# Moving one Ln and Exp of the first half's input norm behind the second half's high parts on ScalarE

## The chip, the cores and the metric

The kernel runs on one core of a Trainium2 chip. The metric is the time of one execution on the device in microseconds (us), as the median of several executions. The engines are TensorE (PE, matrix products), VectorE (DVE), ScalarE (ACT), GpSimd (POOL) and SyncE (SP, which starts transfers). Each works through its own list of instructions in order; between engines there are semaphores.

## The reference

Two transformer blocks run over 512 tokens of width 1024, in float32. At three places the output of a stage is normalised and added to the residual stream, and the new stream is normalised again as the input of the next dense stage. Cut to that:

```python
def rms_norm(x, g):
    xf = x.astype(jnp.float32)
    y = xf * lax.rsqrt(jnp.mean(xf * xf, axis=-1, keepdims=True) + EPS)
    return (y * g.astype(jnp.float32)).astype(x.dtype)

x = x + gate * rmsnorm(mixed @ w_out, g_post)                 # end of the first block
f = swiglu(rms_norm(h, g_ffn1_pre), w_gate, w_up, w_down)     # place A: its input norm
h = h + 0.5 * rms_norm(f, g_ffn1_post)
qkv = rms_norm(h, g_mix_pre) @ w_in                           # place B: its input norm
h = h + rms_norm(mixed @ w_out, g_mix_post)
f = swiglu(rms_norm(h, g_ffn2_pre), w_gate, w_up, w_down)     # place C: its input norm
```

The rest (retention, two attentions of the first block, stick-breaking and banded attention of the second, a gated projection at the end) is not touched.

## The kernel before

**Layout.** Activations lie feature by token: X is 8 tiles of 128 features by 512 tokens. A product in float32 is made of three products of high and low parts (`mm3`, lines 285 to 287): high by high, low by high, high by low. The high part is a rounded copy by ScalarE, the low part the difference by VectorE. Weights come as a stream of 512 KB chunks, four slots deep.

**Halves.** At a join of two stages the tokens are worked in two halves of 256, numbered on through the kernel: t = 0 and 1 at place A (before the first feed-forward), 2 and 3 at place B (before the projection of queries, keys and values of the second block), 4 and 5 at place C (before the second feed-forward). For each half t and each feature tile k:

- VectorE (`next_u`, lines 1106 to 1122), in rounds n: T of tile n = output times root (L1111), X of tile n-1 = new residual (L1115), UL of tile n-2 = low part (L1122). UL of tile k waits for ScalarE's UH of tile k.
- ScalarE (`next_hi`): UH of tile k = X times the gain (the high part), which waits for X of tile k, and then the square of X, into T2 or T3 in turn.
- GpSimd (`sum_n`, L519) adds the squares up, six additions for the half.
- TensorE takes UH and UL of tile k as soon as UL is there (`u_ready`: the wait on `nu_lo`).

**The root of the input norm** is not applied to the input. The products are made of the unnormalised X, and their result is multiplied by the root afterwards (DVE, T6). So the root may come late: `n_stats(t)` on TensorE (L1640 and L1642) sums the squares over the 128 partitions with two products into the half of bank B5 that belongs to t, and `n_rms(t)` on ScalarE makes Ln and then Exp of it into T6.

**TensorE's order** at A and C (`mlp_up`): four weight chunks on the first half (j = 0 to 3, each 24 products of 256 columns), `n_stats(t)`, then the same chunks on the second half, where j = 0 waits tile by tile for UL, with `n_stats(t + 1)` behind j = 1. Then the loop over the remaining chunks with 512 columns. Place B has the same pattern with the first four chunks of the projection.

**ScalarE's order** is written out by hand. `n_rms(t - 1)`, the root of the first half, stands in the middle of the second half's `next_hi`: behind tile 3 at A and C, behind tile 4 at B. It waits for `n_stats` of the first half. The root of the second half follows all eight tiles; at A and C a load of another function table and the first Silu come behind it.

Of the kernel before, what the change touches and what calls it, by code (L numbers as in the profile page):

```python
# [68 lines left out]
def build(nc, a):  # L69
    with ExitStack() as ctx:  # L70
# [77 lines left out]

        TAIL_AT = ((0, 44), (3, 47), (6, 50), (9, 53), (12, 56), (16, 19), (22, 25), (28, 60))
        TAIL_H = [hb(f"TAIL_H{m}", kb, [P, TAIL], F32R) for m, (kb, _) in enumerate(TAIL_AT)]  # L150
        TAIL_L = [hb(f"TAIL_L{m}", kb, [P, TAIL], F32R) for m, (_, kb) in enumerate(TAIL_AT)]

        EP = hb("EP", 0, [P, KT, SEQ])
# [88 lines left out]
        def wait(eng, s, value):  # L242

            if value > 0:
                eng.wait_ge(*((s.sem, s.base + value) if isinstance(s, Event) else (s, value)))
# [37 lines left out]
        def mm3(out, lh, ll, rh, rl, start, stop, **kw):  # L283
# [6 lines left out]
        E = {n: Event(n) for n in (  # L290
            "silu_c converted ada_dot gain_cols x_sq angle sines x_stats u_t u_hi u_lo "
            "y_copy y_sq y_sum y_st y_ln y_rstd y_t x_new nu_hi nu_lo n_sq n_sum n_st n_ln n_rstd half "
            "q_mul q_swap q_rot q_hi q_lo v_hi v_lo k_flat gates "
            "ret_s ret_p ret_hi ret_lo ret_pv gn_x gn_c gn_sq gn_g gn_v gn_ln gn_std gn_m gn_hi gn_lo "
            "cmp_h cmp_silu cmp_dup cmp_kv cmp_kh cmp_kl cmp_bd cmp_st cmp_sc cmp_s cmp_sub cmp_exp cmp_p cmp_t cmp_tc "
            "gate_cols "
            "sb_z sb_m sb_l sb_sp sb_spm sb_sph sb_spl sb_zz sb_p sb_pm sb_hi sb_lo sb_pv "
            "p5_q p5_hi p5_lo p5_vhi p5_vlo rt_tr rt "
# [32 lines left out]
        def cols_of(t):  # L331

            return slice(HALF * (t % 2), HALF * (t % 2) + HALF)
# [278 lines left out]
        def _(act):  # L612
            chain = Chain(act, "act_chain")

            def f(out, in_, func, **kw):
                return nc.scalar.activation(out, in_, func, **kw)  # L616

            def table_set(which):

                nc.scalar.add_instruction(mybir.InstLoadActFuncSet(  # L620
                    name=nc.get_next_instruction_name(), engine=mybir.EngineType.Activation, ins=[], outs=[],
                    act_func_set_id=which))

            def hi_of_weights(d):

                act.wait_ge(raw_here[d % SLOTS], 16 * (d // SLOTS + 1))
                if d in PHASE_OF:
                    phase, m = PHASE_OF[d]
                    hi = kept_weights(phase, m)[0]
                    if phase in ("d1", "d2"):  # L630
                        act.wait_ge(mm, d - m - (8 if m < 5 else 0))
                    f(hi[:, :], RAW[:, d % SLOTS, 0:hi.shape[1]], ACT.Copy).then_inc(w_hi, 1)
                else:
                    f(WH[:, d % SLOTS, :], RAW[:, d % SLOTS, :], ACT.Copy).then_inc(w_hi, 1)
# [20 lines left out]
            def n_rms(t):  # L655

                wait(act, E["n_st"], 2 * t + 2)
                E["n_ln"].mark(f(T[6][:, cols_of(t)], B[5][:, cols_of(t)], ACT.Ln, scale=1.0 / DM, bias=EPS))
                wait(act, E["n_ln"], t + 1)
                E["n_rstd"].mark(f(T[6][:, cols_of(t)], T[6][:, cols_of(t)], ACT.Exp, scale=-0.5))  # L660

            def next_hi(t, k, scale):

                h = cols_of(t)
                wait(act, E["x_new"], 8 * t + k + 1)
                if scale is None:
                    E["nu_hi"].mark(f(UH[:, k, h], X[:, k, h], ACT.Copy))
                    return
                E["nu_hi"].mark(f(UH[:, k, h], X[:, k, h], ACT.Copy, scale=scale[:, k:k + 1]))
                c = t  # L670
                if k >= 2:
                    wait(act, E["n_sum"], 6 * c + max(1, k - 2))
                E["n_sq"].mark(f(T[2 + k % 2][:, h], X[:, k, h], ACT.Square))
# [212 lines left out]
            def mlp_up(d0, n0, t, scale):  # L886

                for k in range(KT):
                    next_hi(t, k, scale)
                    if k == 3:  # L890
                        n_rms(t - 1)
                n_rms(t)
                table_set(SILU_SET)
                for j in range(4):
                    if j >= 2:
                        hi_of_weights(d0 + j + 2)
                    if j % 2 == 0:
                        act.wait_ge(f_g, n0 + j // 2 + 1)
                        f(T[2 + j // 2][:, :], T[j // 2][:, :], ACT.Silu).then_inc(f_s, 1)
                    else:  # L900
                        act.wait_ge(f_h, n0 + j // 2 + 1)
                        f(HH[:, j // 2, :], T[5][:, :], ACT.Copy).then_inc(f_hh, 1)
                c4 = d0 // 4
                with act.Fori(1, 11) as i:
                    for j in range(4):
                        nxt = (j + 2) % 4
                        act.wait_ge(raw_here[nxt], i * 16 + 16 * (c4 + 1 + (j >= 2)))
                        f(WH[:, nxt, :], RAW[:, nxt, :], ACT.Copy).then_inc(w_hi, 1)
                        if j % 2 == 0:
                            act.wait_ge(f_g, i * 2 + (n0 + j // 2 + 1))  # L910
                            f(T[2 + j // 2][:, :], T[j // 2][:, :], ACT.Silu).then_inc(f_s, 1)
                        else:
                            act.wait_ge(f_h, i * 2 + (n0 + j // 2 + 1))
                            f(HH[:, i * 2 + j // 2, :], T[5][:, :], ACT.Copy).then_inc(f_hh, 1)
# [26 lines left out]

            project_out("p2", D_P2, 0, VECS[:, V_F1PRE:V_F1PRE + 8], D_F1)
            mlp_up(D_F1, 0, 1, VECS[:, V_F1PRE:V_F1PRE + 8])
            mlp_down(D_D1, 2, VECS[:, V_MPRE:V_MPRE + 8])
            y_rms(3)
            for k in range(KT):
                next_hi(3, k, VECS[:, V_MPRE:V_MPRE + 8])
                if k == 4:
                    n_rms(2)
            n_rms(3)  # L950


# [97 lines left out]
            for p in range(4):  # L1050
                heads_hi(BDN, p, T[4:6], MBH)
            project_out("p6", D_P6, 4, VEC2[:, V2_F2PRE:V2_F2PRE + 8], D_F2)
            mlp_up(D_F2, 22, 5, VEC2[:, V2_F2PRE:V2_F2PRE + 8])
            mlp_down(D_D2, 6, None)

# [13 lines left out]
            for n in range(17):  # L1069
# [4 lines left out]
                if n < 16:  # L1074
                    m, t = n % 8, 8 + n // 8
# [542 lines left out]
        def _(pe):  # L1618
# [17 lines left out]
            def n_stats(t):  # L1636

                h, c = cols_of(t), t
                wait(pe, E["n_sum"], 6 * c + 6)
                E["n_st"].mark(mat(B[5][:, h], ONES, T[4][:, h], start=True, stop=False))  # L1640
                wait(pe, E["n_sq"], 8 * c + KT)
                E["n_st"].mark(mat(B[5][:, h], ONES, T[3][:, h], start=False, stop=True))  # L1642
# [280 lines left out]
            def mlp_up(phase, d0, n0, t):  # L1923
                for j in range(4):
                    between = None
                    if j == 0:
                        between = lambda: y_stats(t + 1)
                    half_chunk(d0 + j, bank_of(phase, j), *u_in, t, None, between=between,
                               ready=u_ready(t) if j == 0 else None)
                n_stats(t)  # L1930
                for j in range(4):
                    half_chunk(d0 + j, B[j], *u_in, t + 1, mm, ready=u_ready(t + 1) if j == 0 else None)
                    if j == 1:
                        n_stats(t + 1)
                with pe.Fori(1, 11) as i:
                    for j in range(4):
                        pe.wait_ge(w_lo, i * 4 + (d0 + j + 1))
                        pe.wait_ge((f_g, f_u)[j % 2], i * 2 + (n0 + j // 2 - 1))
                        for k in range(KT):
                            ins = mm3(B[j][:, :], wtile(WH, j, k), wtile(WL, j, k), UH[:, k, :], UL[:, k, :], k == 0, k == KT - 1)  # L1940
                        ins.then_inc(mm, 1)
# [41 lines left out]
            for j in range(4):  # L1983
                half_chunk(D_P5 + j, bank_of("p5", j), *u_in, 2, None, ready=u_ready(2) if j == 0 else None,
                           between=(lambda: y_stats(3)) if j == 0 else None)
            n_stats(2)
            for j in range(4):
                half_chunk(D_P5 + j, B[j], *u_in, 3, mm, ready=u_ready(3) if j == 0 else None)
# [252 lines left out]
```

## Time and profile before

| | us |
|---|---|
| median of 3 runs | 1522.67 (1521.61 to 1522.95) |
| the profiled execution's own time | 1521.06 |
| its span in the trace | 1519.3 |
| TensorE busy | 1462.5 (96%) |
| VectorE busy | 838.9 (55%) |
| ScalarE busy | 683.7 (45%) |
| GpSimd busy | 203.6 (13%) |

The span runs from the first to the last instruction; the execution's time is 1.8 us longer. The chain of work that ended last is 82% TensorE, so time is won where TensorE waits or runs at half of its clock. The three places lie at about 420 us (A), 794 us (B) and 1089 us (C) of the span.

### The profile page before, as it was taken

What the parts mean: (1) busy time and instruction counts of PE and PEld (TensorE: products, weight loads), DVE (VectorE), ACT (ScalarE), POOL (GpSimd) and SP (SyncE); (2) the same over time, 40 slices, a digit from 0 to 9 for tenths busy, and PEclk for the clock granted to TensorE, in tenths of its full rate; (3) what the DMA queues carried; (4) which work ended last, traced back from release to release, by engine and by line L of the source; (5) the groups of instructions that cost most, each with busy time, mean ns of one, the idle gap of its engine ahead of it and who ended that gap; (6) DMA issues with size and microseconds to landing.
All of it is one profiled execution on the core that took longest, in us unless ns stands there. A gap on an engine that the chain in (4) does not pass through costs nothing.

```text
span 1519.3 us, 22041 instructions
## 1 busy us (share of the span) xinstructions
PE 1462.5 (96%) x8524; PEld 1234.3 (81%) x8524; DVE 838.9 (55%) x1455; ACT 683.7 (45%) x1302; POOL 203.6 (13%) x319
## 2 busy tenths in 40 slices
PE   7999998999999999999999999989999999999997
PEld 5887875778988888888898777769888888888996
DVE  6688646776654444432285566574754444422374
ACT  4556436676532222221363566676432222322463
POOL 0000000443400000000140223451300000000121
PEclk9999999899999999999999999999999999999998
DMA  9542440004023333333404211503033333332321
GB/s 367 202 152 85 124 153 10 1 2 167 2 84 97 97 97 97 97 97 97 144 10 167 70 56 42 167 16 97 19 107 97 97 97 97 97 111 90 119 84 56
DMA packets 42148, 146.71 MB, mean 97 GB/s; under 512 B 4673, under 2 KB 7121, under 8 KB 41682
## 3 DMA queue, kind: packets, MB, share of 16 engines
q1 hardware_dynamic: 37986, 128.99, 26.5%
q0 software_dynamic: 3072, 15.71, 2.8%
q8 instruction: 54, 0.88, 0.2%
q10 hardware_dynamic: 1008, 0.89, 0.2%
q14 instruction: 28, 0.23, 0.0%
HBM read 141.39 MB, written 4.19 MB: 96 GB/s over the span
## 4 chain that ended last, share of the span: by engine, by line
PE 82%; DVE 10%; ACT 4%; issue 2%; DMA 1%; POOL 0%; DVEq 0%; SPq 0%; ACTq 0%; POOLq 0%
PE B L285 22%; PE B L287 21%; PE B L286 21%; PE CROW_P L285 3%; PE CROW_P L287 3%; PE CROW_P L286 3%; PE B L1772 2%; ACT T L616 1%; PE B L2008 1%; PE CROW_P L1851 1%; DVE WADA L1137 1%; DVE WL L1104 1%; DVE AL L1370 1%; DVE X L1115 1%; PE CROW_P L1751 1%
## 5 line engine op out<-in xcount | busy, mean ns | idle before, releaser
L285 PE MATMUL B<-UH,WH 128*128 128x512 f32 (+1 forms) x1008 | 378.0, 375 | 12.0 <-DVE UL L1122 6.3
L287 PE MATMUL B<-UH,WL 128*128 128x512 f32 (+1 forms) x1008 | 373.9, 371 | 0.0
L286 PE MATMUL B<-UL,WH 128*128 128x512 f32 (+1 forms) x1008 | 373.9, 371 | 0.0
L616 ACT ACTIVATE WH<-RAW 128x1024 fp32r<-128x1024 f32 x174 | 182.6, 1052 | 118.7 <-DMA RAW<-in_stream 110.3
L285 PEld LDWEIGHTS B<-UH,WH 128*128 128x128 f32 x1008 | 191.6, 190 | 47.9 <-DVE UL L1122 8.7
L286 PEld LDWEIGHTS B<-UL,WH 128*128 128x128 f32 x1008 | 191.7, 190 | 31.9
L287 PEld LDWEIGHTS B<-UH,WL 128*128 128x128 f32 x1008 | 191.5, 190 | 32.0
L1104 DVE TENSOR_TENSOR WL<-RAW,WH 128x1024 fp32r<-128x1024 f32 x94 | 116.1, 1240 | 143.8 <-ACT WH L616 143.7
L1447 DVE TENSOR_TENSOR WL<-RAW,WH 128x1024 fp32r<-128x1024 f32 x80 | 98.1, 1226 | 76.7 <-ACT WH L616 73.9
L616 ACT ACTIVATE T<-B 128x256 f32<-128x256 f32 (+5 forms) x186 | 86.3, 464 | 118.0 <-PE B L287 64.3
L510 POOL TENSOR_TENSOR T<-T,T 128x256 f32<-128x256 f32 x60 | 54.7, 912 | 548.8 <-ACT T L616 547.9
L616 ACT ACTIVATE T<-T 128x512 f32<-128x512 f32 (+3 forms) x131 | 68.7, 526 | 131.8 <-DVE T L1451 119.2
L616 ACT ACTIVATE HH<-T 128x512 f32 (+1 forms) x44 | 27.8, 632 | 190.7 <-DVE T L1456 183.8
L286 PE MATMUL B<-HL,WH 128*128 128x512 f32 x192 | 74.8, 390 | 0.0
L285 PE MATMUL B<-HH,WH 128*128 128x512 f32 x192 | 74.8, 390 | 0.0
L287 PE MATMUL B<-HH,WL 128*128 128x512 f32 x192 | 74.8, 389 | 0.0
L285 PE MATMUL B<-UH,KEPT_H 128*128 128x256 f32 (+1 forms) x220 | 66.5, 302 | 1.6 <-DVE KEPT_L L1102 1.6
L1453 DVE TENSOR_TENSOR T<-B,T 128x512 f32<-128x512 f32 x40 | 27.7, 692 | 71.7 <-PE B L287 71.7
L286 PE MATMUL B<-UL,KEPT_H 128*128 128x256 f32 (+1 forms) x220 | 66.0, 300 | 0.0
L287 PE MATMUL B<-UH,KEPT_L 128*128 128x256 f32 (+1 forms) x220 | 65.8, 299 | 0.0
L1370 DVE TENSOR_TENSOR AL<-CROW_P,AH 128x128 fp32r<-128x128 f32 (+3 forms) x96 | 42.7, 484 | 18.1 <-ACT AH L616 17.7
L616 ACT ACTIVATE AH<-CROW_P 128x128 fp32r<-128x128 f32 (+3 forms) x96 | 38.2, 436 | 23.3 <-PE CROW_P L1851 22.6
(419 smaller groups left out, 3161.2 us busy)
## 6 DMA issues: line engine op xcount, KB each, us to landing
RAW<-in_stream SPq DMA_DIRECT2D x202, 512.0 KB, 3.6
WADA<-in_w_ada SPq DMA_DIRECT2D x8, 1024.0 KB, 16.6
RAW<-in_stream SPq DMA_DIRECT2D x16, 384.0 KB, 3.3
WADA<-in_w_ada SPq DMA_DIRECT2D x2, 2048.0 KB, 11.1
W<-in_w POOLq DMA_DIRECT2D x2, 2048.0 KB, 11.7
X<-in_x SPq DMA_DIRECT2D x2, 1024.0 KB, 11.0
DECAY<-in_decay POOLq DMA_DIRECT2D x1, 2048.0 KB, 9.3
X<-in_x POOLq DMA_DIRECT2D x2, 1024.0 KB, 8.2
```

Source lines behind the costliest of these rows:

```text
L285: nc.tensor.matmul(out, lh, rh, start=start, stop=False, **kw)
L286: nc.tensor.matmul(out, lh, rl, start=False, stop=False, **kw)
L287: return nc.tensor.matmul(out, ll, rh, start=False, stop=stop, **kw)
L510: E["y_sum"].mark(nc.gpsimd.tensor_tensor(T[7][:, h], T[8][:, h] if k == 1 else T[7][:, h], T[8 + k % 2][:, h], ALU.add))
L616: return nc.scalar.activation(out, in_, func, **kw)
L1104: tt(WL[:, d % SLOTS, :], RAW[:, d % SLOTS, :], WH[:, d % SLOTS, :], ALU.subtract).then_inc(w_lo, 1)
L1115: E["x_new"].mark(stt(X[:, k, h], T_RING[k % 4][:, h], gain[:, k:k + 1], X[:, k, h], ALU.mult, ALU.add))
L1137: E["ada_dot"].mark(stt(WADA[:, m, :], WADA[:, m, :], 1.0, (CROW_P if m < 2 * KT else CROW)[:, :], ALU.mult, ALU.mult, accum_out=DOTS[:, m ...
L1370: tag["lo"].mark(tt(AL2[:, u % 4, 0:(i + 1) * P], PT_BANK[s][:, 0:(i + 1) * P], AH2[:, u % 4, 0:(i + 1) * P], ALU.subtract))
L1447: tt(WL[:, nxt, :], RAW[:, nxt, :], WH[:, nxt, :], ALU.subtract).then_inc(w_lo, 1)
L1453: tt(T[4][:, :], B[j][:, :], T[6][:, :], ALU.mult).then_inc(f_u, 1)
L1772: ins = [mat(outs[s], fixed[s][x], moving[s][y], start=start and x + y == 0, stop=stop and x == 1) for s in range(2)]
```

## The change

At A and C (`mlp_up` of ScalarE) and at B, `n_rms` of the first half moves from the middle of the second half's tiles to behind the eighth, directly ahead of `n_rms` of the second half. On TensorE `n_stats` of an odd t, which writes the other half of the same bank B5, gets a wait for the Ln of the first half. No instruction is added or removed besides that wait.

```diff
@@ ScalarE, mlp_up (places A and C)
                 for k in range(KT):
                     next_hi(t, k, scale)
-                    if k == 3:
-                        n_rms(t - 1)
+                n_rms(t - 1)
                 n_rms(t)
@@ ScalarE, place B
             for k in range(KT):
                 next_hi(3, k, VECS[:, V_MPRE:V_MPRE + 8])
-                if k == 4:
-                    n_rms(2)
+            n_rms(2)
             n_rms(3)
@@ TensorE, n_stats
                 wait(pe, E["n_sum"], 6 * c + 6)
+                if t % 2 == 1:
+                    wait(pe, E["n_ln"], t)
                 E["n_st"].mark(mat(B[5][:, h], ONES, T[4][:, h], start=True, stop=False))
```

**ScalarE at place A.** UH_51<-X_49 is a high part, T2_177 or T3_178<-X_49 its square, T6_181<-B5 the Ln and T6_181<-T6_181 the Exp of a root. Before, from the square of tile 3 on:

```order
L616 ACTIVATE T3_178<-X_49 128x256 [waits n_sum]
L616 ACTIVATE T6_181<-B5 128x256 [waits n_st]
L616 ACTIVATE T6_181<-T6_181 128x256 [waits n_ln]
L616 ACTIVATE UH_51<-X_49,VECS_205 128x256 [waits x_new]
L616 ACTIVATE T2_177<-X_49 128x256 [waits n_sum]
L616 ACTIVATE UH_51<-X_49,VECS_205 128x256 [waits x_new]
L616 ACTIVATE T3_178<-X_49 128x256 [waits n_sum]
L616 ACTIVATE UH_51<-X_49,VECS_205 128x256 [waits x_new]
L616 ACTIVATE T2_177<-X_49 128x256 [waits n_sum]
```

and now, from the same square to the Exp of the second half's root:

```order
L616 ACTIVATE T3_178<-X_49 128x256 [waits n_sum]
L616 ACTIVATE UH_51<-X_49,VECS_205 128x256 [waits x_new]
L616 ACTIVATE T2_177<-X_49 128x256 [waits n_sum]
L616 ACTIVATE UH_51<-X_49,VECS_205 128x256 [waits x_new]
L616 ACTIVATE T3_178<-X_49 128x256 [waits n_sum]
L616 ACTIVATE UH_51<-X_49,VECS_205 128x256 [waits x_new]
L616 ACTIVATE T2_177<-X_49 128x256 [waits n_sum]
L616 ACTIVATE UH_51<-X_49,VECS_205 128x256 [waits x_new]
L616 ACTIVATE T3_178<-X_49 128x256 [waits n_sum]
L616 ACTIVATE T6_181<-B5 128x256 [waits n_st]
L616 ACTIVATE T6_181<-T6_181 128x256 [waits n_ln]
L616 ACTIVATE T6_181<-B5 128x256 [waits n_st]
```

The Ln, with its wait for `n_st`, stood between the square of tile 3 and the high part of tile 4; now four pairs of high part and square stand there, and both roots follow them. Place C reads the same, and at place B three pairs move ahead in place of four.

**TensorE at place A, the last products of j = 1 and `n_stats(1)`.** Before:

```order
L285 MATMUL B1<-UH_51,WH_56 128x256
L286 MATMUL B1<-UL_52,WH_56 128x256
L287 MATMUL B1<-UH_51,WL_57 128x256
L1640 MATMUL B5<-T4_179,CONST_199 128x256 [waits n_sum]
L1642 MATMUL B5<-T3_178,CONST_199 128x256 [waits n_sq]
L285 MATMUL B2<-UH_51,WH_56 128x256 [waits w_lo]
```

and now:

```order
L285 MATMUL B1<-UH_51,WH_56 128x256
L286 MATMUL B1<-UL_52,WH_56 128x256
L287 MATMUL B1<-UH_51,WL_57 128x256
L1640 MATMUL B5<-T4_179,CONST_199 128x256 [waits n_ln,n_sum]
L1642 MATMUL B5<-T3_178,CONST_199 128x256 [waits n_sq]
L285 MATMUL B2<-UH_51,WH_56 128x256 [waits w_lo]
```

Nothing moves; the first product of the sum waits for `n_ln` too.

## Rows read from the trace of the kernel before

**Rows 1.** The page: busy time of the engines, and the chain that ended last by engine.

```profile
PE 1462.5 (96%) x8524; PEld 1234.3 (81%) x8524; DVE 838.9 (55%) x1455; ACT 683.7 (45%) x1302; POOL 203.6 (13%) x319
...
PE 82%; DVE 10%; ACT 4%; issue 2%; DMA 1%; POOL 0%; DVEq 0%; SPq 0%; ACTq 0%; POOLq 0%
```

**Rows 2.** All waits of PE: operand and line, releaser, us in total, times, longest.

```profile
PE B L285 <- DVE UL L1122: 6.3, 8, 1.5
```

**Rows 3.** Timeline of ScalarE at place A: start, us, engine, line, operation, [idle <- releaser].

```profile
417.33 0.40 ACT L616 ACTIVATE T<-X 128x256 f32<-128x256 f32 x1
421.44 0.38 ACT L616 ACTIVATE T<-B 128x256 f32<-128x256 f32 x1 [3.70 <-PE B L1642]
...
422.17 0.50 ACT L616 ACTIVATE UH<-X,VECS 128x256 fp32r<-128x256 f32 x1
...
432.39 0.38 ACT L616 ACTIVATE T<-B 128x256 f32<-128x256 f32 x1 [5.82 <-PE B L1642]
```

**Rows 4.** Timeline of VectorE at place A.

```profile
417.54 0.47 DVE L1115 SCALAR_TENSOR_TENSOR X<-T,GC,X 128x256 f32<-128x256 f32 x1
417.93 0.96 DVE L1122 SCALAR_TENSOR_TENSOR UL<-X,VECS,UH 128x256 fp32r<-128x256 f32 x1
...
419.15 0.47 DVE L1115 SCALAR_TENSOR_TENSOR X<-T,GC,X 128x256 f32<-128x256 f32 x1
422.70 0.48 DVE L1122 SCALAR_TENSOR_TENSOR UL<-X,VECS,UH 128x256 fp32r<-128x256 f32 x1 [3.08 <-ACT UH L616]
...
426.29 0.69 DVE L1122 SCALAR_TENSOR_TENSOR UL<-X,VECS,UH 128x256 fp32r<-128x256 f32 x1 [0.18 <-ACT UH L616]
```

**Rows 5.** Timeline of GpSimd at place A.

```profile
417.81 0.79 POOL L519 TENSOR_TENSOR T<-T,T 128x256 f32<-128x256 f32 x1 [1.21 <-ACT T L616]
```

**Rows 6.** Timeline of TensorE at place A.

```profile
421.05 0.47 PE L285 MATMUL B<-UH,WH 128*128 128x256 f32 x1
...
425.38 0.39 PE L285 MATMUL B<-UH,WH 128*128 128x256 f32 x1 [1.52 <-DVE UL L1122]
...
431.32 0.60 PE L1640 MATMUL B<-T,CONST 128*128 128x256 f32 x2
...
432.00 0.47 PE L285 MATMUL B<-UH,WH 128*128 128x256 f32 x1
...
437.82 0.28 PE L287 MATMUL B<-UH,WL 128*128 128x256 f32 x1
439.04 0.49 PE L285 MATMUL B<-UH,WH 128*128 128x512 f32 x1 [0.94 <-DVE WL L1104]
```

**Rows 7.** Windows at place A: length, busy PE, PEld, DVE, ACT, POOL, granted clock, DMA share.

```profile
426.00:428.00 2.00, 1.92 (x8) 1.68 (x8) 0.81 (x2) 0.57 (x2) 0.70 (x1) 0.50 0.00 0
428.00:430.00 2.00, 2.00 (x14) 2.00 (x13) 0.00 (x0) 0.00 (x0) 0.00 (x0) 0.70 0.43 90
```

**Rows 8.** Timeline of ScalarE, VectorE and TensorE at place B.

```profile
794.36 0.38 ACT L616 ACTIVATE T<-B 128x256 f32<-128x256 f32 x1 [2.02 <-PE B L1642]
...
792.63 0.95 DVE L1115 SCALAR_TENSOR_TENSOR X<-T,SC,X 128x256 f32<-128x256 f32 x1
...
793.97 0.47 PE L285 MATMUL B<-UH,WH 128*128 128x256 f32 x1
...
801.66 0.60 PE L1640 MATMUL B<-T,CONST 128*128 128x256 f32 x2
```

**Rows 9.** Timeline of VectorE and TensorE at place C.

```profile
1087.72 0.47 DVE L1115 SCALAR_TENSOR_TENSOR X<-T,VECS,X 128x256 f32<-128x256 f32 x1
...
1089.07 0.47 PE L285 MATMUL B<-UH,WH 128*128 128x256 f32 x1
...
1099.77 0.60 PE L1640 MATMUL B<-T,CONST 128*128 128x256 f32 x2
```

**Rows 10.** Waits of PE from 440 us on.

```profile
PE CROW_P L1851 <- DVE AL L1370: 6.4, 10, 2.5
```

**Rows 11.** A window in the attention stage, between B and C.

```profile
1016.00:1024.00 8.00, 6.10 (x52) 5.82 (x53) 4.19 (x9) 3.72 (x8) 4.78 (x4) 0.57 0.23 68
```

## The prediction

> **What bounds the kernel now.** I read the page first. TensorE is busy for 96% of the span and makes up 82% of the chain that ended last [rows 1], so an edit on ScalarE is worth only what it takes from TensorE's waits, or from stretches at half clock. The list of TensorE's waits comes second. One entry is what this edit can touch: 6.3 us in 8 waits of a product for UL, the low part that VectorE makes of the next input [rows 2]. UL waits for the high part UH on ScalarE. So third, the timelines of the three places.
>
> At place A the second half begins on TensorE at 421.05 [rows 6]. ScalarE has squared tile 3 at 417.33 to 417.73 and then stands for 3.70 us, until `n_stats(0)` has let the Ln go at 421.44 [rows 3]. It stands behind TensorE's whole first half, though X of tile 4 was ready at 417.54 + 0.47 = 418.01 [rows 4]. Ln and Exp pass, UH of tile 4 starts at 422.17 [rows 3], UL of tile 4 at 422.70 after 3.08 us of idle time, UL of tile 7 ends at 426.29 + 0.69 = 426.98 [rows 4]. TensorE waits for these tiles (1.52 us for tile 5) [rows 6], and behind these waits its granted clock goes to 0.50, the lower level of 1.2 GHz, in the window from 426, and has a mean of 0.70 in the one from 428 [rows 7]; 2 x 0.50 + 2 x 0.30 = 1.6 us are lost by it.
>
> What that costs is read off one pair of stretches. From the start of the second half to `n_stats(1)` there are 48 products of 256 columns: 431.32 - 421.05 = 10.27 us. The next 48 of the same shape, from 432.00 to the last one, which starts at 437.82 and takes 0.12 until the next could start, need 5.94 us without a wait and at full clock [rows 6]. So **4.33 us** at A are waits and half clock. The same difference is 801.66 - 793.97 - 5.94 = **1.75 us** at B [rows 8] and 1099.77 - 1089.07 - 5.94 = **4.76 us** at C [rows 9]. The most that the edit can win there is 10.84 us.
>
> **The moved root.** Four pairs of UH and square are freed from the wait at A and C, three at B. ScalarE needs 0.50 + 0.40 us for a pair at most [rows 3], under the beat of VectorE, so VectorE sets the pace. Its beat is a round of T, X and UL, from X to X: 419.15 - 417.54 = 1.61 us, with one of the three instructions slowed to 0.96 us [rows 4]. With UH in time, UL of tile 4 comes one beat after that of tile 3: 417.93 + 1.61 = 419.54; tile 5 at 421.15. The last rounds lack T, then X too: between UL of tile 5 and UL of tile 6 lies X alone, between 6 and 7 nothing. At 0.39 us for an instruction (417.93 - 417.54) or 0.88 for a slowed one (0.96 less the overlap of 0.08), with two additions of GpSimd still falling on them, tile 6 starts near 422.3, tile 7 near 423.1 and ends near **423.6**. That is 4.45 us after the start of X of tile 5, at 419.15.
>
> TensorE wants tile 7 of its first chunk 2.7 us after its start: of the 48 products that take 5.94 us, 27 are still to come then, at (437.82 - 432.00) / 47 = 0.12 each. That is 421.05 + 2.70 = 423.75. It is there. Gain at A: 4.3 us, waits and clock together, because TensorE then runs without a pause from the first half on.
>
> At C the same X starts at 1087.72 against TensorE's 1089.07 [rows 9], 1.35 us ahead in place of 1.90. Tile 7 ends at 1087.72 + 4.45 = 1092.17, wanted at 1091.77: 0.4 us stay. Gain 4.76 - 0.4 = 4.4 us. At B, X of tile 5 starts at 792.63 and TensorE's half at 793.97 [rows 8]; only tiles 5 to 7 were held there, for 2.02 us. Tile 7 ends near 797.08, wanted at 796.67: again 0.4 us stay. Gain 1.75 - 0.4, about 1.3 us.
>
> **Why VectorE does not go faster still.** The instruction of 0.96 us at 417.93 lies beside GpSimd's addition of 417.81 to 418.60 [rows 4, 5] and ends 0.29 us behind it; others of the same kind take 0.47. By the Trainium skill, page Advanced Engine Details and Errata, section GPSIMD Details, GpSimd shares a read and a write interface with VectorE and conflicts with VectorE's instructions that have two inputs in SBUF. The trace agrees (0.47 against 0.96 us). This speaks against the change: squares that come earlier send GpSimd's additions into VectorE's rounds. By that rule applied to every instruction the gain is that of the first rival, by the beat of the trace it is the one above.
>
> **The root itself now comes later.** Ln and Exp of the first half come behind the square of tile 7: at A near 423.6, against 421.44 before. Nobody wants them there: VectorE multiplies by the root only after both halves, and it waits for the second half's Exp. Whoever is queued behind them on ScalarE is the second half's Ln, which starts at 432.39 after 5.82 us of idle time [rows 3]; the moved two take 422.17 - 421.44 = 0.73 us together [rows 3], inside that idle time. No transfer is issued among the moved steps and no queue of SP or GpSimd is passed.
>
> **The added wait.** `n_stats(1)` waits for the Ln of the first half, ended by about 424.1 at A. TensorE comes there at 421.05 + 5.94 = 427.0. Cost 0, with about 3 us in hand; behind it on TensorE stand j = 2 and 3 and the whole loop, so if that cover went, each us late would cost 1 us. Bounds: 0 here, and no gain either, since a wait cannot help.
>
> **What is late next.** After A, TensorE waits 0.94 us for the low part of the next weights at 439.04 [rows 6]. Their chain (Ln, Exp, table, Silu, high part, low part) starts with `n_stats(1)` [rows 3, 6], so it moves forward with it and stays 0.94 us. Weight transfers are issued at the end of TensorE's chunks and move too. The gain stays until the end, since behind each place the chain is TensorE's [rows 1].
>
> **Sum.** 4.3 + 1.3 + 4.4 = 10.0 us. The profiled execution took 1521.06; 1511.1 after. Its time is 1.6 below the median of the runs, 1522.67, against which I forecast: **1512.7 us**. Lower bound 10.84 less, 1511.8, and lower only by the clock elsewhere.
>
> **Rivals.**
>
> 1. VectorE is slowed throughout. If all seven instructions from UL of tile 4 on took 0.88, tile 7 would end at 419.54 + 7 x 0.88 = 425.7 at A: 1.95 us of waits remain, and the drop of the clock, 1.6 us [rows 7], may remain. Gain at A 4.33 - 1.95 - 1.6 = 0.8, at C 0.7, at B 0: 1521.2, within 0.2%. For it: [rows 4]. Against: GpSimd has only some 3 additions of 0.79 us left, for three slowed instructions, not seven. A middle form, where one of A and C keeps waits of 1 us and the drop of the clock, gives a gain of 5 to 8: 1514.7 to 1517.7.
> 2. The clock falls elsewhere. All that lies behind A moves by 4 to 10 us. Waits that passed at full clock could bring it down. A drop like that at A costs 1.6 us, and one that vanishes gives as much back. For it: behind A, TensorE has 10 waits of up to 2.5 us for the low parts of the attention weights, 6.4 us in all [rows 10]; one of them is followed by a drop already, a mean of 0.57 over 8 us [rows 11], so 3.4 us lost, which may come out 1.6 shorter or longer. Three more drops: 1517.5. The side where the kernel gets slower is this mechanism with 8 or more new drops, 8 x 1.6 = 12.8 against 10: 1525.5. It decides from 6 drops on, where the gain is gone. Against: the waits do not get longer by the change, and A's drop came behind a row of waits, not one. The Trainium skill says, on the page TensorE: Matmul & The Clock Gate, part 1, that the chip's watch over TensorE's activity runs free and doesn't start with the kernel, so that the same code meets it at another phase. By that, one drop more or less, 1511.1 or 1514.3, is ordinary; no row here shows it.
> 3. The added wait bites: if the squares or sums of the second half came 3 us later than I have them, TensorE would stand at `n_stats`. That would cost gain, not more: n_stats waits for the last squares in any case, 0.4 us before that Ln.
> 4. The edit does nothing, since UL was late for another reason (X itself late). Then tile 4's UL would not have followed 0.02 us behind UH [rows 3, 4]: 422.17 + 0.50 against 422.70. Nearly excluded.
>
> **How the numbers follow.** My forecast with its own range, 1510.5 to 1514.5: 0.74. Middle form of the first rival, 1514.5 to 1518: 0.12. Drops or gains of the clock elsewhere that leave the forecast but stay faster: 0.07. No measurable gain: 0.04. Slower: 0.03. The range from 1509.8 to 1517.0 leaves out about 0.15. A measurement of this kernel can tell about 0.2%, 3 us, from no change. Faster by more than that: 0.93, within it 0.04, slower 0.03.
>
> **What would show it.** In the profile after: no idle time of ScalarE ahead of UH of tile 4 but for X; UL of tile 7 ending about 2.5 us after the start of TensorE's second half at A and 3.1 at B and C (before: 5.9 at A); `n_stats(1)` near 5.95 us behind that start, near 6.35 at B and C; no window below full clock at A and C; the wait of 0.94 us unchanged. I would be wrong if the beat of VectorE from tile 4 on is 2 us or more, if the clock still drops at A or C, or if new drops stand behind them.

## The result

The changed kernel takes 1511.82 us (median of 4 runs, 1510.92 to 1512.90) against 1522.14 us of the kernel before in the same comparison. The ratio is 0.9937 with a 95% interval from 0.9924 to 0.9949: **0.63% faster**, 9.6 us by the ratio, while the medians lie 10.3 us apart. Forecast were 1512.7 us and 10.0 us. The profiled execution's span is 1509.6 us against 1519.3.

The page of the kernel after, in answer to [rows 1]:

```profile
PE 1456.9 (97%) x8524; PEld 1230.8 (82%) x8524; DVE 838.6 (56%) x1455; ACT 683.7 (45%) x1302; POOL 204.3 (14%) x319
...
PE 81%; DVE 12%; ACT 4%; issue 2%; POOL 0%; DVEq 0%; ACTq 0%; POOLq 0%
```

TensorE is busy 5.6 us less and its share of the chain is one point lower.

ScalarE at place A after the change, in answer to [rows 3] (timeline: start, us, engine, line, operation, idle time before it and what ended that):

```profile
417.27 0.40 ACT L616 ACTIVATE T<-X 128x256 f32<-128x256 f32 x1
417.98 0.51 ACT L616 ACTIVATE UH<-X,VECS 128x256 fp32r<-128x256 f32 x1 [0.31 <-DVE X L1113]
...
422.48 0.51 ACT L616 ACTIVATE UH<-X,VECS 128x256 fp32r<-128x256 f32 x1 [0.46 <-DVE X L1113]
422.90 0.40 ACT L616 ACTIVATE T<-X 128x256 f32<-128x256 f32 x1
423.20 0.36 ACT L616 ACTIVATE T<-B 128x256 f32<-128x256 f32 x1
...
428.17 0.38 ACT L616 ACTIVATE T<-B 128x256 f32<-128x256 f32 x1 [4.16 <-PE B L1642]
```

The square of tile 3 at 417.27 is followed by the high part of tile 4 at 417.98, as soon as X is there; it was 422.17 before. The first half's Ln stands at 423.20, behind all tiles, and the second half's at 428.17, after 4.16 us of idle time.

VectorE, in answer to [rows 4], and TensorE, in answer to [rows 6], both at A; then TensorE's first product of the loop behind it:

```profile
417.47 0.47 DVE L1113 SCALAR_TENSOR_TENSOR X<-T,GC,X 128x256 f32<-128x256 f32 x1
...
419.09 0.96 DVE L1113 SCALAR_TENSOR_TENSOR X<-T,GC,X 128x256 f32<-128x256 f32 x1
...
422.37 1.35 DVE L1120 SCALAR_TENSOR_TENSOR UL<-X,VECS,UH 128x256 fp32r<-128x256 f32 x2
```

```profile
420.99 0.47 PE L285 MATMUL B<-UH,WH 128*128 128x256 f32 x1
...
423.38 0.39 PE L285 MATMUL B<-UH,WH 128*128 128x256 f32 x1
...
427.11 0.60 PE L1640 MATMUL B<-T,CONST 128*128 128x256 f32 x2
...
434.82 0.49 PE L285 MATMUL B<-UH,WH 128*128 128x512 f32 x1 [0.94 <-DVE WL L1102]
```

The low parts of tiles 6 and 7 lie in one row that ends at 423.72; before, tile 7 ended at 426.98. TensorE's half starts at 420.99, its sum at 427.11: 6.12 us in place of 10.27. The product at 423.38 is the first of tile 6; it starts 0.17 us behind the one ahead of it, where 0.12 is the pace, so TensorE barely waits any more. The wait of 0.94 us for the next weights has not changed. The two windows behind, in answer to [rows 7], are at full clock (the last three columns are the granted clock, the share of the DMA engines and GB/s):

```profile
424.00:426.00 2.00, 2.00 (x19) 2.00 (x18) 0.00 (x0) 0.01 (x1) 0.00 (x0) 1.00 0.39 55
426.00:428.00 2.00, 2.00 (x16) 1.89 (x15) 0.00 (x0) 0.00 (x0) 0.00 (x0) 1.00 0.55 215
```

Places B and C, in answer to [rows 8, 9], TensorE at B, VectorE at B, TensorE at C:

```profile
789.74 0.47 PE L285 MATMUL B<-UH,WH 128*128 128x256 f32 x1
...
792.69 0.39 PE L285 MATMUL B<-UH,WH 128*128 128x256 f32 x1 [0.44 <-DVE UL L1120]
...
796.41 0.60 PE L1640 MATMUL B<-T,CONST 128*128 128x256 f32 x2
```

```profile
788.40 0.96 DVE L1113 SCALAR_TENSOR_TENSOR X<-T,SC,X 128x256 f32<-128x256 f32 x1
...
791.68 1.35 DVE L1120 SCALAR_TENSOR_TENSOR UL<-X,VECS,UH 128x256 fp32r<-128x256 f32 x2
```

```profile
1083.39 0.47 PE L285 MATMUL B<-UH,WH 128*128 128x256 f32 x1
...
1086.34 0.39 PE L285 MATMUL B<-UH,WH 128*128 128x256 f32 x1 [0.45 <-DVE UL L1120]
...
1090.07 0.60 PE L1640 MATMUL B<-T,CONST 128*128 128x256 f32 x2
```

B takes 6.67 us in place of 7.69, C 6.68 in place of 10.70. Each keeps one wait of 0.44 or 0.45 us.

The span falls apart into stretches that can be compared one by one. In this table, made from TensorE's rows of each trace, A, B and C are the 48 products from the start of a second half to its sum; "A to B" and "B to C" lie between, "to end" behind C.

| kernel | start of A | A | A to B | B | B to C | C | to end | start of A to end |
|---|---|---|---|---|---|---|---|---|
| before | 421.05 | 10.27 | 362.65 | 7.69 | 287.41 | 10.70 | 419.53 | 1098.25 |
| after | 420.99 | 6.12 | 362.63 | 6.67 | 286.98 | 6.68 | 419.53 | 1088.61 |
| e1_a_and_c | 420.89 | 6.14 | 362.64 | 7.68 | 286.58 | 6.67 | 419.50 | 1089.21 |
| e2_b_alone | 425.50 | 10.67 | 362.65 | 6.69 | 286.56 | 10.23 | 419.60 | 1096.40 |
| e4_filled_wait | 421.11 | 9.35 | 362.65 | 7.68 | 287.55 | 9.35 | 419.51 | 1096.09 |
| e3_short_sums | 420.18 | 5.94 | 362.66 | 5.94 | 286.82 | 5.94 | 419.52 | 1086.82 |
| e5_late | 421.13 | 6.12 | 362.66 | 6.65 | 286.96 | 6.66 | 419.52 | 1088.57 |
| e6_later | 421.39 | 9.49 | 362.71 | 10.04 | 287.10 | 10.04 | 419.93 | 1099.31 |
| e8_behind_5 | 420.31 | 6.42 | 362.63 | 6.69 | 287.31 | 6.67 | 419.57 | 1089.29 |
| e7_weights_first | 422.86 | 6.14 | 361.45 | 6.66 | 286.34 | 6.67 | 418.38 | 1085.64 |

From the start of A's second half to the end the change saves 9.64 us: 4.15 at A, 1.02 at B, 4.02 at C, 0.43 between B and C, 0.02 in the rest.

### The profile page after: what moved, and what is told of

Read it like the earlier page. It is cut to its first block, busy times and chain, and to the rows that moved or that the text cites. A ratio compares the mean times of both kernels' runs of the same rounds, so it can differ in the third digit from the quotient of the medians.

```text
span 1509.6 us, 22044 instructions
## 1 busy us (share of the span) xinstructions
PE 1456.9 (97%) x8524; PEld 1230.8 (82%) x8524; DVE 838.6 (56%) x1455; ACT 683.7 (45%) x1302; POOL 204.3 (14%) x319
## 4 chain that ended last, share of the span: by engine, by line
PE 81%; DVE 12%; ACT 4%; issue 2%; POOL 0%; DVEq 0%; ACTq 0%; POOLq 0%
PE B L285 21%; PE B L286 21%; PE B L287 21%; PE CROW_P L285 3%; PE CROW_P L286 3%; PE CROW_P L287 3%; PE B L1772 2%; PE B L2008 1%; DVE WADA L1135 1%; PE CROW_P L1851 1%; ACT T L616 1%; DVE X L1113 1%; DVE UL L1120 1%; DVE WL L1102 1%; DVE T L1109 1%
## 5 line engine op out<-in xcount | busy, mean ns | idle before, releaser
L1456 DVE TENSOR_TENSOR HL<-T,HH 128x512 f32 x40 | 27.7, 693 | 36.6 <-ACT HH L616 36.6
## 6 DMA issues: line engine op xcount, KB each, us to landing
X<-in_x SPq DMA_DIRECT2D x2, 1024.0 KB, 10.7
```

What stands on the lines that cost most here:

```text
L1456: tt(HL[:, i * 2 + j // 2, :], T[5][:, :], HH[:, i * 2 + j // 2, :], ALU.subtract).then_inc(f_hl, 1)
```

## The experiments

**Each place by itself.** Theory: every place gives back its own waits and its own drop of the clock. Rival: the gain is one place's, or the clock's elsewhere. First the change at A and C alone; the hunk of `mlp_up` and the wait on TensorE stay, and at B:

```diff
                 next_hi(3, k, VECS[:, V_MPRE:V_MPRE + 8])
-            n_rms(2)
+                if k == 4:
+                    n_rms(2)
             n_rms(3)
```

> The root is moved at places A and C only; place B is as before. Theory (each place gives back its own waits and clock drop): the profile after gives 4.15 us at A and 4.02 at C, read as the shorter way from the start of TensorE's second half to its sum, so 8.2 us less than before, a ratio near 0.9946. Rival (the gain is one place's, or the clock's elsewhere): clearly less than 7 or more than 9.5 us.

Measured: 1512.68 us, ratio 0.9933 (0.9915 to 0.9950). TensorE at B in that trace:

```profile
789.67 0.47 PE L285 MATMUL B<-UH,WH 128*128 128x256 f32 x1
...
793.62 0.38 PE L285 MATMUL B<-UH,WH 128*128 128x256 f32 x1 [1.13 <-DVE UL L1121]
...
797.35 0.60 PE L1641 MATMUL B<-T,CONST 128*128 128x256 f32 x2
```

B takes 7.68 us with its old wait, A and C take 6.14 and 6.67 as in the changed kernel. A and C give 4.13 + 4.03 = 8.16 us, as the theory says. From the start of A to the end it is 9.04 us less, since the stretch from B to C came out 0.83 us shorter. That goes with a shorter drop of the clock there, a mean of 0.79 over 8 us where [rows 11] have 0.57:

```profile
1010.00:1018.00 8.00, 5.26 (x45) 4.64 (x45) 3.21 (x7) 4.27 (x9) 3.98 (x5) 0.79 0.21 56
```

The times by themselves would not decide: by the ratio it is 10.2 us, with an interval from 7.6 to 12.9, which holds the theory's 8.2 as well as the rival's "more than 9.5". The stretches decide.

Then the change at B alone:

```diff
                     next_hi(t, k, scale)
-                n_rms(t - 1)
+                    if k == 3:
+                        n_rms(t - 1)
                 n_rms(t)
```

> The root is moved at place B only. Theory: 1.0 us less than before (7.69 against 6.67 us in the profile after), a ratio near 0.9993, too small to be told from no change in the time, but to be read in the trace as 6.7 us from the start of the second half to the sum; the drops of the clock behind A and C stay. Rival (the moved root at B costs, as it comes later): 7.7 us or more in that stretch.

Measured: B takes 6.69 us in the trace, 1.00 less, as expected, and A and C keep 10.67 and 10.23 us. The time was 1518.37 us, ratio 0.9973 (0.9958 to 0.9989). That is 4 us less than before where 1.0 was expected, and the trace doesn't show such a gain: in the profiled execution, which took 1523.62 us, the way from A to the end is only 1.85 us shorter, 0.85 of it between B and C. The mean granted clock of each run tells more. The two runs of e2_b_alone at 0.983 took 1523.62 and 1523.90 us, those of the kernel before at the same clock 1524.71 to 1525.37; at 0.988 and 0.989 it is 1517.18 to 1519.08 against 1519.97 to 1520.19. So at a like clock the change at B is worth some 1 to 2 us, and the rest of the 4 us is that seven of its nine runs had a clock of 0.987 or more, against five of the nineteen of the kernel before. Why it was so stays open; the last section shows where executions differ by that much.

**What the clock has to do with it.** The kernel before, but TensorE is kept busy inside its long wait:

```diff
+            def filled(t, d):
+                def ready(k):
+                    if k == 5:
+                        keep_clock(6, WH[:, d % SLOTS, 0:SEQ], B[6])
+                    wait(pe, E["nu_lo"], 8 * t + k + 1)
+                return ready
...
-                    half_chunk(d0 + j, B[j], *u_in, t + 1, mm, ready=u_ready(t + 1) if j == 0 else None)
+                    half_chunk(d0 + j, B[j], *u_in, t + 1, mm, ready=filled(t + 1, d0) if j == 0 else None)
```

> The kernel before, with the root where it was, but TensorE is given six products of 512 columns into an unused bank between tiles 4 and 5 of the second half's first chunk at A and C, about 6 x 0.23 = 1.4 us inside its wait of 1.52 us. Theory (the clock falls because TensorE waits there): no window under full clock behind A and C, the 48 products take about 8.7 us in place of 10.3 and 9.1 in place of 10.7, in all 3.2 us less than before, ratio 0.998. Rival (the clock would fall anyway, or for another reason): the drop stays and the time is the same or up to 0.5 us longer.

Measured: 1518.93 us, ratio 0.9970 (0.9960 to 0.9980). By the times that is 4 to 5 us, more than the 3.2 expected and than the 2.16 that the way from A to the end shows; the surplus is not explained, as at e2_b_alone. TensorE at A (the filling, tiles 5, 6 and 7, the sum) and two windows behind it:

```profile
423.76 1.53 PE L1648 MATMUL CROW_P<-WH 128*128 128x512 f32 x6
425.46 0.39 PE L285 MATMUL B<-UH,WH 128*128 128x256 f32 x1 [0.16 <-DVE UL L1122]
...
426.25 0.38 PE L285 MATMUL B<-UH,WH 128*128 128x256 f32 x1 [0.17 <-DVE UL L1122]
...
427.12 0.38 PE L285 MATMUL B<-UH,WH 128*128 128x256 f32 x1 [0.25 <-DVE UL L1122]
...
430.46 0.60 PE L1640 MATMUL B<-T,CONST 128*128 128x256 f32 x2
```

```profile
426.00:428.00 2.00, 1.57 (x11) 1.29 (x11) 0.89 (x2) 0.66 (x2) 0.79 (x1) 1.00 0.00 0
428.00:430.00 2.00, 2.00 (x19) 2.00 (x19) 0.00 (x0) 0.00 (x0) 0.00 (x0) 1.00 0.59 143
```

The six products fill the wait, 0.16 us of it is left ahead of tile 5, and both windows are at full clock where [rows 7] shows 0.50 and 0.70. So the drop comes from TensorE's waiting, as the theory says. But the stretch falls to 9.35 us, not to the expected 8.7: at A the drop cost 10.27 - 9.35 = 0.92 us, at C 10.70 - 9.35 = 1.35. The remaining 9.35 - 5.94 = 3.41 us are waits, the filled one among them. I had counted the granted clock's whole shortfall, 1.6 us, as lost; a part of it falls where TensorE waits for tiles 6 and 7 anyway. At full clock these waits are 0.17 and 0.25 us (the rows above). In the kernel before they stand at C, where the clock falls only by tile 7,

```profile
1094.19 0.39 PE L285 MATMUL B<-UH,WH 128*128 128x256 f32 x1 [0.17 <-DVE UL L1122]
...
1095.07 0.58 PE L285 MATMUL B<-UH,WH 128*128 128x256 f32 x1 [0.26 <-DVE UL L1122]
```

while at A, where it falls ahead of tile 6, the trace shows no wait at tiles 6 and 7: the slower products fill that time. 0.17 + 0.26 = 0.43 us is as much as the drop costs more at C than at A. So the price depends on the moment of the drop: in e2_b_alone the two figures stand the other way round, 10.67 us at A and 10.23 at C.

**What sets VectorE's beat.** The changed kernel, with GpSimd's additions of five of the second half's tiles cut to 16 columns; it leaves most of those sums out:

```diff
                 h, c = cols_of(t), t
                 wait(pool, E["n_sq"], 8 * c + k + 1)
...
+                if t % 2 == 1 and k > 1:
+                    h = slice(h.start, h.start + 16)
                 E["n_sum"].mark(nc.gpsimd.tensor_tensor(T[4][:, h], T[2][:, h] if k == 1 else T[4][:, h],
```

> The changed kernel; GpSimd's additions of the squares of tiles 2 to 6 of the second halves go over 16 of the 256 columns only, so most of those sums of squares are left out. They are no longer beside VectorE's instructions. Theory (VectorE's beat is set by GpSimd's additions, 0.96 in place of 0.47 us for one instruction each): the beat from X to X falls from 1.61 to about 1.15 us, tile 7 is ready in time at B and C too, the stretch takes 5.95 us at all three places, so 1.4 to 1.7 us less than the changed kernel. Rival (VectorE is slowed by ScalarE or by its own writes): the beat stays at 1.6 us and the time is that of the changed kernel.

Measured: 1511.22 us, ratio 0.9926 (0.9907 to 0.9946); its runs go from 1508.79 to 1514.76, too far apart to show 1.5 us, so the trace has to. An addition on GpSimd, and X of tiles 4 and 5 and the last low part on VectorE, at A, where TensorE's half starts at 420.18:

```profile
418.68 0.28 POOL L521 TENSOR_TENSOR T<-T,T 128x16 f32<-128x16 f32 x1 [0.85 <-ACT T L618]
```

```profile
417.27 0.47 DVE L1115 SCALAR_TENSOR_TENSOR X<-T,GC,X 128x256 f32<-128x256 f32 x1
...
418.40 0.47 DVE L1115 SCALAR_TENSOR_TENSOR X<-T,GC,X 128x256 f32<-128x256 f32 x1
...
420.24 0.49 DVE L1122 SCALAR_TENSOR_TENSOR UL<-X,VECS,UH 128x256 fp32r<-128x256 f32 x1 [0.18 <-ACT UH L618]
```

The addition takes 0.28 us in place of 0.79 [rows 5], no instruction of VectorE takes 0.96 any more, the beat is 418.40 - 417.27 = 1.13 us in place of 1.61, and tile 7 is ready 0.55 us after TensorE's start. All three stretches take 5.94 us, exactly the figure without a wait. So what the change leaves at B and C, 0.73 and 0.74 us, and the 0.18 at A, goes back to GpSimd's additions, beside which VectorE's instructions are slowed. The three places give 1.65 us together, as expected, and from A to the end it is 1.79.

**How late the root may be.** The changed kernel with copies on ScalarE ahead of the moved root, at all three places, 5 and then 15 of them:

```diff
+            def idle(n):
+                for _ in range(n):
+                    chain.done(f(T[5][:, 0:HALF], X[:, 0, 0:HALF], ACT.Copy))
...
+                idle(5)
                 n_rms(t - 1)
                 n_rms(t)
...
+            idle(5)
             n_rms(2)
             n_rms(3)
```

> The changed kernel, with 5 copies of 256 columns on ScalarE, each waited for, ahead of the moved root at all three places: about 2 to 2.5 us. Theory (TensorE comes to the sum of the second half 3.5 us after the Ln of the first half at A, 3.5 at B and C): the delay is hidden, the time is that of the changed kernel within 0.3 us. Rival (the late root costs at once): 2 us more at each place, 6 in all.

> The same with 15 copies, about 6.5 to 7 us. Theory: the Ln comes some 3 to 3.5 us after TensorE reaches the sum, which waits for it by the added wait, so about 3 us more at each place, 9 to 10 in all, plus up to 1.6 us a place if the clock falls: as slow as the kernel before, or slower by up to 5 us. Rival (nobody waits for that Ln): the time of the changed kernel.

Measured with 5: 1511.35 us, ratio 0.9937 (0.9922 to 0.9953), and stretches of 6.12, 6.65 and 6.66 us. With 15: 1524.20 us, ratio 1.0016 (1.0002 to 1.0030). ScalarE at A with 5 copies (they share a row with the last square), then ScalarE and TensorE at A with 15:

```profile
423.04 2.52 ACT L616 ACTIVATE T<-X 128x256 f32<-128x256 f32 x6
425.59 0.39 ACT L616 ACTIVATE T<-B 128x256 f32<-128x256 f32 x1
...
428.31 0.39 ACT L616 ACTIVATE T<-B 128x256 f32<-128x256 f32 x1 [1.89 <-PE B L1648]
```

```profile
423.30 7.02 ACT L616 ACTIVATE T<-X 128x256 f32<-128x256 f32 x16
430.35 0.39 ACT L616 ACTIVATE T<-B 128x256 f32<-128x256 f32 x1
...
430.88 0.67 PE L1646 MATMUL B<-T,CONST 128*128 128x256 f32 x2 [3.21 <-ACT T L616]
```

With 5 copies the Ln comes at 425.59 and costs nothing. With 15 it comes at 430.35, and TensorE's sum of the second half waits for it 3.21 us, 3.20 at B and 3.21 at C. The stretches are 3.37 us longer than in the changed kernel at each place, 10.1 in all, of 10.7 in the whole. The granted clock stays at 1.00 in every window behind A, but falls behind B and C, to a mean of 0.79 over the 8 us from 803.60 and from 1100.70: the same wait of 3.2 us brings a drop at two places and none at the third. The added wait is real, its cover ends where forecast, and behind it a us costs about one. The root's own lateness costs nothing by itself.

**Where behind the wait.** The root behind tile 5 at all three places:

```diff
                     next_hi(t, k, scale)
-                n_rms(t - 1)
+                    if k == 5:
+                        n_rms(t - 1)
                 n_rms(t)
```

> The root of the first half is put behind tile 5 at all three places, not behind tile 7. In the profile after, the square of tile 5 ends at 420.9 at A, and the first half's sum is there at 421.4. Theory (what costs is that ScalarE stands while X is ready): the Ln waits 0.5 us, Ln and Exp take 0.8, the high part of tile 6 comes 0.9 us later than in the changed kernel, TensorE waits 0.3 to 0.9 us more at each place: 1 to 2.5 us slower than the changed kernel, 7 to 8.5 faster than before. Rival (any place between tiles is as good once the wait is gone): the time of the changed kernel.

Measured: 1511.54 us, ratio 0.9939 (0.9924 to 0.9955). ScalarE and VectorE at A, where TensorE's half starts at 420.31:

```profile
420.70 0.38 ACT L616 ACTIVATE T<-B 128x256 f32<-128x256 f32 x1 [0.48 <-PE B L1644]
...
421.44 0.50 ACT L616 ACTIVATE UH<-X,VECS 128x256 fp32r<-128x256 f32 x1
```

```profile
421.97 0.48 DVE L1122 SCALAR_TENSOR_TENSOR UL<-X,VECS,UH 128x256 fp32r<-128x256 f32 x1 [0.19 <-ACT UH L616]
422.67 0.67 DVE L1122 SCALAR_TENSOR_TENSOR UL<-X,VECS,UH 128x256 fp32r<-128x256 f32 x1 [0.22 <-ACT UH L616]
```

The steps came as I had them: the Ln waits 0.48 us, the high part of tile 6 starts 1.13 us behind TensorE's start, against 421.20 - 420.99 = 0.21 in the changed kernel. The price did not: A takes 6.42 us, 0.30 more, B and C 6.69 and 6.67, nothing more. My estimate of 1 to 2.5 us was wrong, and the gain of 9.3 us by the ratio is more than the 7 to 8.5 I had. The late high parts also make their squares late, GpSimd's additions leave VectorE's rounds, and the low part of tile 6 takes 0.48 us, where in the changed kernel the low parts of tiles 6 and 7 took 1.35 us together. What VectorE waits for ScalarE it mostly gains on GpSimd. So the gain lies in leaving the long wait, not in the exact place behind it.

**A faster version.** The waits of 0.94, 0.85 and 0.93 us behind the three places are for the first weights of the next loop. ScalarE and VectorE stand idle ahead of the second half's root, so their part in these weights can go there:

```diff
@@ ScalarE, mlp_up
                 n_rms(t - 1)
+                hi_of_weights(d0 + 4)
                 n_rms(t)
...
-                    if j >= 2:
+                    if j == 3:
                         hi_of_weights(d0 + j + 2)
@@ VectorE, project_out
+                lo_of_weights(up + 4)
                 wait(dve, E["n_rstd"], t + 2)
@@ VectorE, mlp_up
-                    if j >= 2:
+                    if j == 3:
                         lo_of_weights(d0 + j + 2)
@@ place B, ScalarE (and the same with lo_of_weights on VectorE)
-                if c >= 2:
+                if c == 1:
+                    hi_of_weights(D_P5 + 4)
+                if c >= 3:
                     hi_of_weights(D_P5 + c + 2)
```

> The changed kernel, with the high and low part of the first weights of the next loop made while ScalarE and VectorE stand idle ahead of the second half's root (A and C), or one step earlier (B). Theory (the waits of 0.94, 0.93 and 0.85 us for these weights are only an order on ScalarE and VectorE): they vanish, 2.0 to 2.7 us less than the changed kernel; the root comes 0.5 us later at A and C, and its chain has that much room behind it. Rival (the chain through Silu is what the loop waits for next): the waits turn into others for the second chunk and the time stays.

Measured: 1509.44 us, ratio 0.9921 (0.9907 to 0.9935), the fastest of all kernels here that compute everything. In the same comparison e5_late and e8_behind_5 took 1511.35 and 1511.54, 1.9 and 2.1 us more; the intervals of the ratios overlap, so here too the stretches are the firmer evidence. ScalarE and VectorE at A:

```profile
429.90 1.06 ACT L616 ACTIVATE WH<-RAW 128x1024 fp32r<-128x1024 f32 x1 [4.00 <-DMA RAW<-in_stream]
430.87 0.37 ACT L616 ACTIVATE T<-B 128x256 f32<-128x256 f32 x1
...
430.99 1.23 DVE L1105 TENSOR_TENSOR WL<-RAW,WH 128x1024 fp32r<-128x1024 f32 x1 [5.39 <-ACT WH L616]
```

The high part waits for its transfer and delays the second half's Ln: it starts 430.87 - 429.00 = 1.87 us behind the start of TensorE's sum, where it was 428.17 - 427.11 = 1.06 in the changed kernel, so 0.8 us later and not 0.5. The low part is ready at 432.2, and TensorE takes it at 435.62 without a wait. The three waits are gone and no other takes their place: A to B 1.18 us shorter, to the end 1.15, B to C 0.64, and from the start of A to the end 2.97 us less than the changed kernel. The theory held; the rival (the chain through Silu) did not show.

## Why the prediction was right

**The bound and the most that could be won.** The 5.94 us without a wait were read right: three stretches of e3_short_sums took exactly that.

**The moved root.** Forecast 4.3 + 1.3 + 4.4 = 10.0 us; measured 4.15 + 1.02 + 4.02 = 9.19, and 0.43 by a shorter stretch between B and C. Each term was a little too large, for two reasons that lie in TensorE's side of the comparison. At A, tile 7 ended at 423.72 where 423.6 was forecast, so the walk along VectorE's beat was right in its end (the low part of tile 4 came 0.43 us later than in the walk, at 419.97, because X of tile 5 took 0.96 us). But I compared tile 7 alone with TensorE. At B it was tile 6 that came late: its low part, the first of the two in the row at 791.68, released the product at 792.69, which by TensorE's own pace was wanted 18 products behind 789.74, at 792.08. That is 0.61 us late; the row shows 0.44 because it counts from the end that the profile gives the product ahead, 0.28 us behind its start, while the next can start after 0.12. Besides, the first product behind a wait takes 0.22 us until the next starts and not 0.12, and so the stretches lost 0.73. So "0.4 us stay" should have been 0.73 at both places, and "it is there" at A 0.18.

**The time itself.** The forecast of 1512.7 us came within 0.9 us of the median. That is in part luck: the runs of one kernel differ by several us for a reason ahead of place A (last section), the stretches give 9.64 us and the medians 10.3. What bears the forecast out is the stretches, term by term. The 0.43 us between B and C were in no term, and nothing here shows their cause.

**The split into waits and clock** was mis-sized, though the sum was not touched: 1.6 us were put down to the clock at A, and the filled wait shows 0.92 at A and 1.35 at C.

**VectorE's beat** was right, and its cause is shown by e3_short_sums: with short additions the 0.96 us became 0.47. The first rival, all seven instructions slowed, did not come; two of them were slowed, as in the walk, and X of tile 5 ahead of them.

**The later root and the added wait** cost nothing, with TensorE at the sum 427.11 - 423.56 = 3.55 us behind the end of the Ln (forecast about 3). The third rival is real beyond that: 15 copies show it.

**What is late next.** 0.94 us behind A, as forecast; e7_weights_first shows that it was a matter of order.

**The clock elsewhere.** No new drop came. The old one between B and C is there after the change too, with the same mean of 0.57 over 8 us as [rows 11]:

```profile
1010.00:1018.00 8.00, 5.49 (x48) 5.12 (x46) 3.57 (x8) 3.87 (x9) 4.64 (x4) 0.57 0.20 68
```

## What to carry to other kernels

On an engine that works in order, a wait for a result that nobody needs soon holds all that stands behind it: look for the engine's own idle time, see whether its next input was ready, and move the step that waits behind the work that the bound engine wants. Then check the cover of what is now late, and check every tile of a chain against the moment at which it is wanted, not only the last. An engine that becomes free sooner also starts others sooner, and these may slow the very chain that was sped up.

## What the runs showed of the hardware

**Part of a clock drop is free.** 1.6 us of missing clock at A cost 0.92 us of time and 1.35 at C; the difference is the waits of 0.17 and 0.26 us that the slower products fill at A.

**A wait does not bring a drop each time.** In e6_later the wait of 3.2 us is the same at all three places, and the clock falls behind two of them.

**Most of the spread between these traces lies ahead of place A.** The kernels here are the same up to there. Yet A's second half started between 420.18 and 425.50 us, while the stretch from A to B took 362.63 to 362.71 in nine of the ten kernels. Busy time and clock over the first 420 us, and the start of A's second half, of e2_b_alone and then of e8_behind_5:

```profile
0.00:420.00 420.00, 395.99 (x2576) 321.14 (x2577) 284.12 (x583) 237.03 (x491) 69.52 (x97) 0.96 0.33 114
...
425.50 0.47 PE L285 MATMUL B<-UH,WH 128*128 128x256 f32 x1
```

```profile
0.00:420.00 420.00, 393.38 (x2618) 321.23 (x2619) 289.22 (x592) 239.25 (x497) 71.69 (x100) 0.99 0.32 114
...
420.31 0.47 PE L285 MATMUL B<-UH,WH 128*128 128x256 f32 x1
```

The granted clock has a mean of 0.96 in the one and 0.99 in the other, and the place is reached 5.2 us later. Added up over windows of 2 us, the clock missing ahead of A is 17.1 us in the one and 5.1 in the other: 12 us more for 5.2 us of time, so here too more than half of it is free, if nothing but the clock differs. Between B and C one more such difference lies, of up to 1 us. The drop there comes in two lengths: 3.4 us of missing clock in the kernel before, the changed one, e4_filled_wait and e8_behind_5, with stretches of 286.98 to 287.55 us, and 1.7 in e1_a_and_c, e2_b_alone, e3_short_sums and e5_late, with 286.56 to 286.96. (e7_weights_first has the long one and 286.34, but without the wait behind B; e6_later has the short one and a second behind B.) What decides it from one execution to the next was not tried. It means that a median of few runs of this kernel can be off by several us, as at e2_b_alone, while the stretch from A to B, behind the places where the clock differs, repeats to 0.1 us in the traces.
